# Four stage changes and the end of a 66-block transformer program, done by halves of the 512 tokens

## What is computed

```python
def rmsnorm_2(x, g):
    y = xf * lax.rsqrt(jnp.mean(xf * xf, axis=-1, keepdims=True) + EPS)
    return y * g
def swiglu_2(h, w_gu, w_down):
    g, u = jnp.split(h @ w_gu, 2, axis=-1)
    return (jax.nn.silu(g) * u) @ w_down
def sandwich(x, fn, g_pre, g_post, shift, scale, gate, res_w):
    h = modulate_2(rmsnorm_2(x, g_pre), shift, scale)
    y = rmsnorm_2(fn(h), g_post)
    return x + res_w * gate[:, None, :] * y
```

## Time and profile before

| | us |
|---|---|
| median of 3 runs (lowest, highest) | 2894.25 (2890.47, 2895.38) |
| the profiled execution | 2892.19 |
| its span, first to last instruction | 2890.4 |
| PE busy | 2781.9 |
| DVE busy | 1615.8 |
| POOL busy | 1100.4 |
| ACT busy | 995.2 |

### The profile page before, as it was taken

The page is one execution under the profiler, slowest core; times in us unless marked ns, Lnnn a source line. Parts: engine busy times, 40 slices in busy tenths (PEclk is TensorE's granted clock), DMA queues, the critical chain, the costliest instruction groups (busy, mean ns, idle before and its releaser), DMA issues.

```text
span 2890.4 us, 40334 instructions
## 1 busy us (share of the span) xinstructions
PE 2781.9 (96%) x15008; PEld 2325.2 (80%) x15008; DVE 1615.8 (56%) x2590; ACT 995.2 (34%) x1693; POOL 1100.4 (38%) x566
## 2 busy tenths in 40 slices
PE   8989999999999999999999999999989989999998
PEld 6778878888888789978888788887778767788886
DVE  6788875555555668765555633444463764522223
ACT  3267231211112357532222322223362762322222
POOL 1333223333333253344455344444334334344433
PEclk7999999999999999999999999999999989999999
DMA  5222523232322122334444334443223222132221
GB/s 231 77 52 78 197 87 118 102 116 88 122 80 102 38 74 60 114 118 171 152 152 167 102 124 152 140 150 129 83 74 102 73 73 87 59 102 94 95 93 58
DMA packets 88689, 309.74 MB, mean 107 GB/s; under 512 B 10881, under 2 KB 11009, under 8 KB 87169
## 3 DMA queue, kind: packets, MB, share of 16 engines
q1 hardware_dynamic: 88578, 308.24, 32.0%
HBM read 287.23 MB, written 2.10 MB: 100 GB/s over the span
## 4 chain that ended last, share of the span: by engine, by line
PE 83%; DVE 11%; ACT 3%; issue 2%; DMA 1%; POOL 1%; SPq 0%; DVEq 0%; ACTq 0%; POOLq 0%
PE ps L301 71%; PE ps L1434 3%; PE ps L1422 2%; PE ps L502 2%; PE ps L1404 2%; DVE negm L1483 1%; PE ps L358 1%; DVE ps L609 1%; PE ps L1628 1%; DVE xl L616 1%; DVE rec L1842 1%; PE ps L1218 1%; PE ps L1407 1%; DVE r_g L1834 1%; DVE y L609 1%
## 5 line engine op out<-in xcount | busy, mean ns | idle before, releaser
L278 POOL TENSOR_TENSOR w_lo<-raw,w_hi 128x1024 fp32r<-128x1024 f32 x367 | 932.6, 2550 | 1433.0 <-ACT w_hi L272 1433.0
L272 ACT ACTIVATE w_hi<-raw 128x1024 fp32r<-128x1024 f32 x367 | 383.8, 1057 | 1330.4 <-PE ps L301 1229.4
L301 PE MATMUL ps<-n_hi,w_hi 128*128 128x512 f32 x1504 | 593.9, 395 | 12.0 <-DVE n_lo L1873 4.9
L301 PE MATMUL ps<-n_lo,w_hi 128*128 128x512 f32 x1504 | 586.7, 390 | 0.0
L301 PE MATMUL ps<-n_hi,w_lo 128*128 128x512 f32 x1504 | 586.6, 390 | 0.0
L828 DVE TENSOR_TENSOR y<-y,ps 128x512 f32<-128x512 f32 (+1 forms) x440 | 270.6, 632 | 264.3 <-PE ps L301 264.2
L301 PEld LDWEIGHTS ps<-n_hi,w_hi 128*128 128x128 f32 x1504 | 283.4, 188 | 81.0 <-issue 11.7
L347 DVE CUSTOM_DVE_ANT_0 dump<-modraw 128x1024 f32<-128x1024 f32 x196 | 335.2, 1710 | 12.4 <-DMA modraw<-mod_stream 7.6
L783 DVE TENSOR_TENSOR ps<-ffn_silu,ps 128x512 f32<-128x512 f32 x110 | 68.5, 641 | 472.7 <-PE ps L301 458.2
L301 PEld LDWEIGHTS ps<-n_lo,w_hi 128*128 128x128 f32 x1504 | 283.4, 188 | 60.0 <-issue 2.7
L301 PEld LDWEIGHTS ps<-n_hi,w_lo 128*128 128x128 f32 x1504 | 283.2, 188 | 59.2
(11 more groups left out here) (280 smaller groups left out, 3747.5 us busy)
## 6 DMA issues: line engine op xcount, KB each, us to landing
raw<-w_stream SPq DMA_DIRECT2D x367, 512.0 KB, 4.2
modraw<-mod_stream SPq DMA_DIRECT2D x152, 512.0 KB, 3.8
mod_pair<-mod_first SPq DMA_DIRECT2D x7, 1024.0 KB, 12.5
l_qs<-l_q_hi SPq DMA_DIRECT2D x32, 128.0 KB, 2.3
l_qs<-l_q_lo SPq DMA_DIRECT2D x32, 128.0 KB, 2.4
l_qs<-l_q_hi SPq DMA_DIRECT2D x16, 192.0 KB, 2.9
l_qs<-l_q_lo SPq DMA_DIRECT2D x16, 192.0 KB, 3.5
xl<-x_in SPq DMA_DIRECT2D x1, 2048.0 KB, 7.6
```

Source lines behind the costliest of these rows:

```text
L272: nc.scalar.activation(w_hi[:, c % RING, :], raw[:, c % RING, :], ACT.Copy).then_inc(hi_ready, 1)
L278: nc.gpsimd.tensor_tensor(w_lo[:, c % RING, :], raw[:, c % RING, :], w_hi[:, c % RING, :].bitcast(F32), ALU.subtract).then_inc(lo_ready, 1)
L301: mm = nc.tensor.matmul(out, w[a], x[b][:, off:off + n], start=first and i == 0, stop=last and i == 2)
```

## The change

It touches the four places where 512 tokens go from one stage to the next (`l1_out` to `l1_ffn`, `l1_ffn` to `s_ffn1`, `s_ffn1` to `s_in`, `s_out` to `s_ffn2`) and the end. Each is done by halves of 256 tokens: the last four weight blocks (of a feed-forward stage the last gate, up and two output blocks; of an output stage blocks 4 to 7), the post norm, the addition, the pre norm, and the first four blocks of the next stage (`first_four`), with the second half's products of the old stage beside the first half's norm. The squares become the weights of a matmul with one column of ones (`half_sum`), so that a token's sum lies on its partition; DVE sums over the chunks (`half_total`), ACT takes the root and DVE the reciprocal of two columns, and PE spreads the result over all rows by a product with the identity (`half_wide`). The pairwise additions, the transposes and, at these places, `keep_warm` are gone.

The first group of a feed-forward stage leaves the loop; DVE copies its outputs instead of adding them, and POOL's memset of `y` is gone. The bias and vectors of the modulation are made before the last group. In `l1_out` the plan of modulation blocks per weight block changes.

Core of the diff:

```diff
-PASSES = ["l0_mix_pre", "l0_mix_post", "l0_ffn_pre", "l0_ffn_post", "l1_mix_pre", "l1_mix_post",
...
+PASSES = ["l0_mix_pre", "l0_mix_post", "l0_ffn_pre", "l0_ffn_post", "l1_mix_pre"]
+HALVES = ((0, S // 2), (S // 2, S // 2))
+HC = S // 2
...
-    WARM = {1: (18, 16), 2: (24, 20)}
+    WARM = {2: (24, 20)}
...
+    def half_sum(squares_, bank, k):
+        for t in range(2):
+            mm = nc.tensor.matmul(half(bank)[:, KC * t + k:KC * t + k + 1], squares_[:, k % 4, t * P:(t + 1) * P],
+                                  ones[:, 0:1], start=True, stop=True)
+        return mm
+    def half_total(bank):
+        sums = half(bank)
+        return nc.vector.reduce_sum(sums[:, 16:18], sums[:, 0:16].rearrange("p (t k) -> p t k", t=2), AX.X)
+    def half_root(bank):
+        sums = half(bank)
+        return nc.scalar.activation(sums[:, 18:20], sums[:, 16:18], ACT.Sqrt, scale=1.0 / D, bias=eps_col[:, 0:1])
+    def half_wide(bank, row):
+        for t in range(2):
+            mm = nc.tensor.matmul(half(bank)[:, t * P:(t + 1) * P], half_rinv[:, row, t:t + 1].to_broadcast([P, P]), ident,
+                                  start=True, stop=True)
+        return mm
...
+    def first_four(pe, h, c0):
...
+        for e in range(2):
+            for k in range(KC):
+                pe.wait_ge(h_half, chunks_before(h, e) + k + 1)
+                for b in range(2):
+                    mm = step(e, b, k)
...
+                if e == 0 and k == 3 and h in (0, 3):
+                    post_spread(pe, h, 1)
+            for b in range(2, 4):
+                pe.wait_ge(lo_ready, c0 + b + 1)
+                for k in range(KC):
+                    mm = step(e, b, k)
+                    if e == 0 and k % 2 == 1:
+                        pre_sum(pe, h, 1, 4 * (b - 2) + k // 2)
...
+            if e == 0:
+                pre_spread(pe, h, 1)
...
+    def last_halves_pe(pe, f, h, c, g):
...
+        part_block(0, 0, HALF_GATE[0])
+        part_block(0, 1, HALF_UP[0])
+        pe.wait_ge(hid_ready, CREDIT + f["m"] + 2 * g + 1)
+        part_block(1, 0, HALF_GATE[1])
...
+        outs(0, None, beside_first)
+        part_block(1, 1, HALF_UP[1], {k: lambda i=i: post_sum(pe, h, 0, i) for k, i in ((1, 4), (3, 5), (5, 6), (7, 7))})
+        outs(1, lambda: post_spread(pe, h, 0), beside_second)
...
+        post_sum(pe, h, 1, 5)
+        pre_sum(pe, h, 0, 3)
+        post_sum(pe, h, 1, 6)
+        pre_sum(pe, h, 0, 4)
+        post_sum(pe, h, 1, 7)
+        for k in range(5, KC):
+            pre_sum(pe, h, 0, k)
+        post_spread(pe, h, 1)
+        pre_spread(pe, h, 0)
...
+    def halves_out_pe(pe, name, h):
...
+        for n in range(4):
+            pe.wait_ge(lo_ready, c0 + n + 1)
+            block(n)
+        for n in range(4, 8):
+            pe.wait_ge(lo_ready, c0 + n + 1)
+            pe.wait_ge(y_half, chunks_before(h, 0) + n - 3)
+            block(n, 0, {4: {}, 5: {3: post(0, 0), 7: post(0, 1)}, 6: {3: post(0, 2), 7: post(0, 3)}, 7: {3: post(0, 4), 7: post(0, 5)}}[n])
+        copied(4)
+        block(4, 1, {1: post(0, 6), 3: post(0, 7), 6: lambda: post_spread(pe, h, 0)})
...
-    OUT_MODS_1 = [2, 2, 2, 1, 1, 1, 1, 0]
+    OUT_MODS_1 = [3, 3, 2, 2, 0, 0, 0, 0]
...
-            nc.gpsimd.memset(f["y"][:, :, 0:n], 0.0).then_inc(y_zero, 1)
...
-        out_pe(pe, "l1_out", (n_hi, n_lo), "l1_mix_post")
-        keep_warm(pe, "l1_ffn_pre", 0)
-        norm_pe(pe, "l1_ffn_pre")
-        keep_warm(pe, "l1_ffn_pre", 1)
-        ffn_pe(pe, l1_ffn)
-        sums_after(pe, "l1_ffn_post")
...
+        halves_out_pe(pe, "l1_out", 0)
+        ffn_pe(pe, l1_ffn, lambda pe, f, c, g: last_halves_pe(pe, f, 1, c, g))
+        ffn_pe(pe, s_ffn1, lambda pe, f, c, g: last_halves_pe(pe, f, 2, c, g))
```

More of the change, by code:

```diff
@@ new lines, in ffn_groups, with in_block @@
+        step(n0, 0, (0, 0, 0))
+        with eng.Fori(0, (NG - 3) // 2) as i:
+            for turn_ in range(2):
+                step(n0 + 6 * (1 + turn_), i * 12, (1 + turn_, i * 2, i))
+        step(n0 + 6 * (NG - 2), 0, (NG - 2, 0, 0))
+        last(n0 + 6 * (NG - 1), NG - 1)
+    def in_block(pe, f, c, d, bank, buf):
+        pe.wait_ge(lo_ready, c + 1 + d)
+        project(f["x"][0], f["x"][1], c, [(bank(buf, si), off, n) for si, (off, n) in enumerate(f["segs"])]
+                ).then_inc(w_used, 1)
@@ L754, in ffn_act, with step @@
         ffn_hidden_hi(act, f, 0, 0, None, 0)
-        def step(c, d, group, last):
+        def step(c, d, group):
             g, gd = group[:2]
@@ new lines, in step, with last_group_act, last_halves_act, silu @@
+            split_hi(act, c + RING + 3, d)
+            split_hi(act, c + RING + 4, d)
+            split_hi(act, c + RING + 5, d)
+            ffn_hidden_hi(act, f, 2 * g + 2, 2 * gd, c + 6, d)
+        ffn_groups(act, f, step, lambda c, g: last_groups(act, f, c, g))
+    def last_group_act(act, f, c, g):
+        split_hi(act, c + RING)
+        ffn_silu(act, f, c, 0, 1)
+        split_hi(act, c + RING + 1)
+        ffn_hidden_hi(act, f, 2 * g + 1, 0, c, 0)
+        root_ahead()
+    def last_halves_act(act, f, h, slot, c, g):
+        j = f["index"] - 1
+        def silu(e):
+            off, n = HALVES[e]
+            if e == 0:
+                act.wait_ge(half_in, 2 * j + 1)
+            else:
+                act.wait_ge(w_used, c + 1)
+            nc.scalar.activation(f["silu"][:, 1, off:off + n], half(HALF_GATE[e]), ACT.Silu).then_inc(half_silu, 1)
+        def hidden_hi(e):
+            off, n = HALVES[e]
+            act.wait_ge(half_hid, 2 * j + e + 1)
+            nc.scalar.activation(f["hi"][:, 1, off:off + n], half(HALF_UP[e]), ACT.Copy).then_inc(half_hid_hi, 1)
+        act.wait_ge(w_used, c)
+        silu(0)
+        hidden_hi(0)
+        silu(1)
+        root_ahead()
+        split_hi(act, c + RING)
+        for k in range(KC):
+            post_square(act, h, 0, k)
+        hidden_hi(1)
+        post_root(act, h, 0)
+        split_hi(act, c + RING + 1)
+        for k in range(KC):
+            post_square(act, h, 1, k)
+            if k >= 1 and h < 4:
+                pre_square(act, h, 0, k - 1)
+        if h == 4:
+            post_root(act, h, 1)
+            return
+        pre_square(act, h, 0, KC - 1)
+        post_root(act, h, 1)
+        pre_root(act, h, 0)
+        split_hi(act, c + RING + 2)
+        pre_high(act, h, 0, 0, slot)
+        pre_high(act, h, 0, 1, slot)
+        split_hi(act, c + RING + 3)
+        for k in range(2, KC):
+            pre_high(act, h, 0, k, slot)
+        second_half_act(act, h, slot)
@@ L773, in ffn_last_blocks, with second_half_act @@
+    def second_half_act(act, h, slot):
+        for k in range(KC):
+            pre_square(act, h, 1, k)
+        pre_root(act, h, 1)
+        for k in range(KC):
+            pre_high(act, h, 1, k, slot)
     def ffn_last_blocks(f):
@@ L2044, in _ @@
             stage(name)
-        for k in range(KC):
-            x_chunk(sp, before("s2_post", "_post") + 1, k)
-            sp.dma_start(A["out"][:, k, :], xl[:, k, :]).then_inc(out_stored, 16)
-        sp.wait_ge(out_stored, 16 * KC)
+        for e, (off, n) in enumerate(HALVES):
+            for k in range(KC):
+                x_half_done(sp, 4, e, k)
+                sp.dma_start(A["out"][:, k, off:off + n], xl[:, k, off:off + n]).then_inc(out_stored, 16)
+        sp.wait_ge(out_stored, 32 * KC)
     @block.scalar
```

652 lines of the change are left out of this document (485 added, 167 removed).

## The result

The changed kernel takes 2919.05 us (median of 6 runs, 2914.35 to 2929.25) against 2894.82 us of the kernel before beside it: ratio 1.008, interval 1.0055 to 1.0105. It is slower, by 24.2 us; 2917 was forecast, with 2897 to 2938 as the range. The profiled execution took 2918.53 us, its span is 2916.7.

A forecast was written before the change was run, and what follows sets the result against it. PE, busy 96% of the span, was taken as the bound. Terms 6.4 + 3.8 + 3.8 + 2.1 + 0.4 + 7.0 = 23.5 us on 2892.2 gave 2915.7, with 2.1 for the median 2917 us; range 2897 to 2938.

The forecast's parts named there:

- change B, C without the clock: Changes from l1_ffn to s_ffn1 and from s_ffn1 to s_in: 27.8 us against 24.0 before, +3.8 us each.
- change D without the clock: Change from s_out to s_ffn2: 27.1 us against 24.9 before, +2.1 us.
- change A without the clock and the plan: Change from l1_out to l1_ffn: 27.1 us against 24.9 before, +2.1 us.
- the end: Last group and post norm by halves: last addition 1.0 us later, smaller last store credited 0.6, so +0.4 us.
- Squares as columns: PE's column sums at the changes: four passes of 0.11 us, 0.45 us a sum, 32 per change, +14.4 us.
- Rival A: Column sums: loads hide under the previous pass, a sum costs 0.23 us, 31 us less, total 2886 us; chance 0.11.
- The waits: PE waiting in each feed-forward change: 0.6, 2.95, 2.9 for DVE's pace and 2.65 between the halves, 9.1 us.
- the modulation ahead of the last group: DVE's modulation bias and vectors before the last group's first product: hidden by half 1's gate block and filled products.
- The plan in l1_out: Modulation blocks 3, 3, 2, 2 delay weight loads; PE wants block 6 at 1229.9, has it at 1233.5: +4.3 us (0 to 8).
- The clock: Falls to 0.50 at the changes: +3.0 us each in two feed-forward changes, 0.5 in out changes, +7 (0 to 16).
- Rival B: At the changes: everything as walked but no low clock, total 2910 us; chance 0.22.
- Rival C: l1_out starves by 8 us, POOL's splits hold up chunks, each change loses 2 more, total 2930 us; chance 0.12.

The follow-up runs named there:

- wide_and_fill: Changed kernel with the edits of wide_sums and fill_waits together, sums still four passes; 2916.86 us, ratio 1.0058 to the kernel before.
- mods_spread: Changed kernel with l1_out's modulation blocks planned 2, 1, 1, 1 ahead of blocks 0 to 3 and again ahead of blocks 4 to 7; 2912.85 us.
- single_pass: Changed kernel with squares and ones column in float32r, two columns, so a column sum is two passes instead of four; 2893.01 us.
- weights_first: Changed kernel with SP issuing l1_out's loads of weight blocks 5, 6 and 7 ahead of the modulation loads; 2915.56 us.
- fill_waits: Changed kernel with small 128-column matmuls where PE waits: 4 before the next stage's first product, 4 and 6 around the spread between its halves; 2912.25 us.
- wide_sums: Changed kernel with each column-sum pass moving 120 columns of ones instead of 1; 2912.23 us.
- double_sums: Changed kernel with each column-sum matmul issued twice; 3026.46 us.
- before_single: Kernel before with float32r squares and ones for its 512-token sums, one pass instead of two, keep-warm matmuls kept; 2884.45 us.
- before_no_warm: Kernel before without its keep-warm matmuls at the changes of 512 tokens; 2903.30 us, ratio 1.0019.

## Why the prediction was right

The direction and its cause were foreseen: PE's column sums use up most of what the halves save, and waits and clock do the rest. The number is nearer than the terms are. They sum to 23.5 us, the stretches grew by 28.1, and the medians, which carry the wander ahead of A, differ by 24.2; that 2919 came so close to 2917 is partly luck. (By the prediction's own figures, 2915.7 and 2.1, it should have read 2917.8.) The terms, each beside its measurement; wide_and_fill stands for the changed kernel with its clock held, mods_spread for it with l1_out's plan mended.

| term | predicted | measured |
|---|---|---|
| a column sum | 0.45 us | 0.44 (1.16 - 0.72) |
| 256-column product | 0.120 | 0.120 |
| end of the second half's up block to the next stage's first product, clock held | 17.85 | 17.64, 17.65 |
| pace of DVE, two blocks by chunks | 7.2 | 7.0 |
| gap between the halves, with its spread | 3.1 | 3.05 (1674.84 to 1677.89) |
| change B, C without the clock | +3.8 each | +3.8, +4.0 |
| change D without the clock | +2.1 | +1.3 |
| change A without the clock and the plan | +2.1 | +2.6, some clock in it |
| modulation plan in l1_out | +4.3 (0 to 8) | +7.9 |
| the end | +0.4 | +0.4 clock held, +1.2 |
| clock | +7 (0 to 16) | +9 |

The measured terms add up to 29.0 and not 28.1, because part of A's low clock is in two of them. The sign that the prediction named, l1_ffn's first product to s_ffn1's at some 390 us, reads 390.2 (1266.75 to 1656.96).

*Squares as columns.* The forecast rested on the price of a one-column pass behind a fresh load of 128x128 fp32, read from the first modulation's row. That row was the right neighbour: the ten sums take 5.93 us, partly at low clock, and passes stand 0.11 us apart. Rival A would have had a sum at half the price or less. single_pass shows what that would have given: level with before, where A's own working put the balance ("passes the old one at about 0.25 us per sum"; 0.22 gives 0.9994). The gain that A named came nearly true (31 us forecast; 30.2 in the stretches, 26.0 in the medians), its 2886 did not (2893.01): the terms without A had come to 28.1 us and not 23.5, and single_pass begins A 4.7 us later than the changed kernel does. Nor did its clock hold (78.3 us low). The Trainium skill (TensorE: Matmul & The Clock Gate, Back-to-back issue gap), from which the prediction took 0.1 us a sum, gives the floor of 25 ns for a lone matmul and says itself that at small sizes this leaves out the loading of weights. That agrees with the 0.11 us of a pass here; the prediction's 0.1 us a sum and 2875 left this out.

*The waits.* The walk through the queues came out within 0.3 us in the feed-forward changes (17.64 for 17.85; 3.05 for 3.1) and 0.6 too long in s_out (22.6, from 2502.74 to the next stage's first product at 2525.33, for 23.15), because every duration in it was a row of the trace and every hand-over was counted. The claim that the modulation ahead of the last group costs nothing nearly held: DVE is busy with it for 5.5 us in B, and the first half's output products with their four sums take 8.20 us there against 7.45 in C, 0.75 more. Those 0.6 us are most of what D cost less than forecast (1.3 against 2.1).

*The plan in l1_out* is the step that was mis-sized. SP's issues of blocks 6 and 7 were forecast for 1224.6 and 1230 and came at 1224.43 and 1229.31, with A starting 1.7 us earlier than in the trace that the forecast was made from. But what I followed from there, "PE wants block 6", was the lesser part. The squares on ACT stand behind the weight splits, and the copies on DVE behind the modulation blocks; with the weights early, PE waited longer (weights_first). The lateness had two sources, DVE's queue and the loads, and DVE's alone was enough. And each wait took the clock down with it. The term is 7.9 instead of 4.3, just inside its bound of 8; its mechanism was half of the true one.

*The clock.* Low at both handovers of B and C, as forecast for the first ("a stretch of about 8 us"); the second fall, between the halves, was not forecast. Of the forecast 3.0 each for B and C, 4.8 and 2.2 were measured, and B's figure moves by 2.3 us between executions of the same code, as said above. The two cheap terms, D and the end, err by less than 1 us each and in opposite directions.

Rival B (the clock holds) is refuted by the windows. Rival C had the starvation at 8 and each change 2 worse: the first half came true (7.9), the second only in B (8.6 against 3.8 + 3.0), and the time lies nearer to 2917 than to 2930.

What stays open: why l0_ffn runs at two paces at the same clock, which no run of this study addressed; and whether the halves bring a few us once sum and clock are mended.

## What to carry to other kernels

Cutting a stage in halves to fill a gap multiplies the small operations around it, so price the smallest one first: here a sum of 0.44 us, 144 times, made a kernel slower that is level at 0.22, and the same cheaper sum in the old order gave as much as the whole rebuilt order. Count what stands ahead of an operation on its own engine, not only what it reads: a load brought forward gives nothing if the consumer waits for a copy that is queued behind other work. Where PE does tiny passes under fresh weights, let them move more columns: here up to 120 cost nothing and kept the clock longer. Small matmuls where PE waits did the same (fill_waits). Before comparing medians a few us apart, look whether a stretch that both kernels share took the same time.

## What the runs showed of the hardware

- A pass whose weights are a fresh 128x128 fp32 tile takes 0.11 us at full clock whether it moves 1 or 120 columns. More columns also keep the clock up longer: the time at 0.50 falls from 88.1 to 57.9 us in wide_sums.
- A row of one-column passes does not hold the clock although PE is busy all the time: it fell at 1649.5 and 2042.0 inside the ten sums of B and C (changed kernel). Eight of them to six products of 256 columns let it fall in B of double_sums (1.49 instead of 0.82 us for the products) but did not in C, for 13 us.
- float32r takes a sum of 512 columns from 0.86 to 0.23 us, more than the two passes that become one account for: a fp32 pass of 512 columns was 0.43 us, the single one 0.23.
- DVE's modulation block with both inputs in SBUF takes 1.21 to 1.23 us where POOL is idle meanwhile (87 of 196 in the changed kernel), and 2.13 on average and up to 3.44 us where POOL works (109); the row at 1228.88 above, from weights_first, is such a one. The 20 blocks with one input in PSUM take 1.20 to 1.22 us with POOL at work or not. The Trainium skill (SBUF — State Buffer, Who interferes with whom) has a DVE instruction with two SBUF inputs contend with a POOL one that reads SBUF; the rows agree. A plan that counts such blocks at 1.2 us each is short.
- Beside POOL's memset of `y` (128x4096, 3.51 us) at l1_ffn's end DVE's copy of 128x8 into `vec_b` takes 3.39 us, in the kernel before (at 1645.12), before_single and before_no_warm alike; at s_ffn1's end, with no memset, it takes 0.16 to 0.17. This cost the kernel before some 0.2 us, because the sums on PE ended only at 1647.55 and the transposition behind them took 0.92 us instead of 0.72. In before_single, whose sums are shorter, it took 1.59. The prediction put the memset's going at nothing; that held for the kernel before, and would not for one with cheaper sums.
- Products of the same form, back to back at clock 1.00, came at two paces in different profiled executions: 578 or 568 in 100 us of l0_ffn.
